# Projections issued in four parts with an attention unit behind three of them, another order of chunks, and one modulation row summed by VectorE

## The reference

```
mod   = silu(cond) @ w_mod + b_mod          # six rows of 2048 for each of the two conditions: SH1 SC1 G1 SH2 SC2 G2
h     = rms_norm(x) * (1 + SC1) + SH1
z     = h @ w_in                            # columns: queries, keys, values of the head groups A, B, C
o     = attention(A: 6 heads), windowed attention with a sink(B: 6 heads), latent attention(C: 4 heads)
x1    = x + G1 * (concat(o) @ w_o)
h2    = rms_norm(x1) * (1 + SC2) + SH2
y     = x1 + G2 * experts(h2)               # top-1 group, top-2 of its 8 experts; each expert silu(h2@w1)*(h2@w3) @ w2
```

## Time and profile before

| | us |
|---|---|
| median of 3 runs | 1692.17 (1691.69 to 1693.72) |
| the profiled execution | 1693.61 |
| its span, first to last instruction | 1691.8 |
| PE busy, whole span | 1591.9 (94%) |
| DVE busy | 690.1 (41%) |
| ACT busy | 263.7 (16%) |
| POOL busy | 106.1 (6%) |

### The profile page before, as it was taken

One profiled execution on the slowest core, in us unless ns is written; L12 is line 12 of the kernel. 1 busy time (PEld: TensorE's weight loads), 2 busy tenths in 40 slices (PEclk: granted clock), 3 DMA queues, 4 the chain that ended last, 5 costly groups with the idle time before them and its releaser, 6 DMA issues.

```text
span 1691.8 us, 18209 instructions
## 1 busy us (share of the span) xinstructions
PE 1591.9 (94%) x6671; PEld 655.4 (39%) x6716; DVE 690.1 (41%) x1361; ACT 263.7 (16%) x706; POOL 106.1 (6%) x192
## 2 busy tenths in 40 slices
PE   5999999999999999999999998999999999998998
PEld 3455555544434444443332332333233233233332
DVE  3113232113245893344444345345344433544444
ACT  2004221112133000011101101110110111111010
POOL 1022100100020100000000000000000000000000
PEclk9999999999999999999999999999999999999999
DMA  9992643535199765599999999999999999999995
GB/s 394 420 385 120 230 193 119 215 109 213 54 368 410 275 264 221 203 366 426 427 429 428 428 425 428 428 424 428 427 426 428 425 424 427 428 428 423 428 427 237
DMA packets 60526, 581.94 MB, mean 344 GB/s; under 512 B 9129, under 2 KB 10121, under 8 KB 16105
## 3 DMA queue, kind: packets, MB, share of 16 engines
q1 hardware_dynamic: 53120, 557.34, 79.6%
q0 software_dynamic: 6064, 23.22, 3.6%
q10 hardware_dynamic: 1296, 0.77, 0.2%
HBM read 584.06 MB, written 7.05 MB: 349 GB/s over the span
## 4 chain that ended last, share of the span: by engine, by line
PE 68%; DMA 17%; DVE 4%; issue 2%; ACT 1%; SPq 0%; POOL 0%; ACTq 0%
PE bank L1298 24%; DMA ring<-in_w 17%; PE bank L1046 14%; PE bank L1208 7%; PE bank L1025 7%; DVE r L1794 2%; PE bank L920 2%; PE bank L1331 2%; PE bank L1133 2%; PE bank L1257 2%; PE bank L1280 1%; PE bank L1108 1%; PE bank L1194 1%; PE bank L1116 1%; PE bank L1313 1%
## 5 line engine op out<-in xcount | busy, mean ns | idle before, releaser
L1298 PE MATMUL bank<-ring,r 128*64 128x512 f32 x1920 | 469.6, 619 | 45.5 <-DMA ring<-in_w 45.5
L1298 PEld LDWEIGHTS bank<-ring,r 128*64 128x64 f32 x1920 | 129.6, 140 | 303.3 <-issue 303.3
L1046 PE MATMUL bank<-ring,r 128*128 128x384 f32 (+1 forms) x672 | 242.4, 519 | 0.0
L2014 DVE TENSOR_TENSOR bank<-bank,r 128x512 f32<-128x512 f32 x180 | 125.9, 700 | 266.2 <-PE bank L1208 266.2
L1331 PE MATMUL bank<-ring,mod_row 128*64 128x512 f32 x896 | 195.4, 593 | 7.9 <-ACT mod_row L1547 7.9
L1025 PE MATMUL bank<-ring,r 128*128 128x512 f32 x384 | 170.0, 595 | 0.0
L1046 PEld LDWEIGHTS bank<-ring,r 128*128 128x128 f32 x672 | 126.9, 191 | 103.7 <-issue 44.7
L1208 PE MATMUL bank<-r 128*128 128x512 bf16 x495 | 137.6, 382 | 7.2 <-issue 7.2
L2016 DVE TENSOR_TENSOR r<-r,bank 128x512 f32<-128x512 f32 x180 | 123.7, 687 | 6.2
L1331 PEld LDWEIGHTS bank<-ring,mod_row 128*64 128x64 f32 x896 | 75.4, 137 | 118.2 <-issue 107.9
L1208 PEld LDWEIGHTS bank<-r 128*128 128x128 bf16 x540 | 38.0, 97 | 167.4 <-DVE r L2016 97.4
(11 more groups left out here) (281 smaller groups left out, 1238.4 us busy)
## 6 DMA issues: line engine op xcount, KB each, us to landing
ring<-in_w SPq DMA_DIRECT2D x180, 2048.0 KB, 17.8
ring<-in_w_mod SPq DMA_DIRECT2D x64, 1024.0 KB, 11.8
ring<-in_w_first SPq DMA_DIRECT2D x32, 1024.0 KB, 25.9
ring<-in_w SPq DMA_DIRECT2D x19, 1024.0 KB, 9.7
ring<-in_w_o SPq DMA_DIRECT2D x16, 1024.0 KB, 6.2
r<-mod_d POOLq DMA_DIRECT2D x8, 1024.0 KB, 8.0
ring<-in_w_aq SPq DMA_DIRECT2D x8, 768.0 KB, 11.4
ring<-in_w_bq SPq DMA_DIRECT2D x8, 768.0 KB, 13.0
```

The source lines that it names most:

```text
L1046: mm = pe.matmul(acc[acc_of(a)][:, 0:w], h_t[:, k, t * P:(t + 1) * P], wu[:, j, :], start=(k == 0), stop=(k == KD - 1))
L1298: mm = pe.matmul(ps[64 * c:64 * c + 64, :], xg_t[:, j, 64 * c:64 * c + 64], big_cut(slot_of(u), (8, 512))[:, j % 8, :], start=(j == 0), st ...
L2014: v.tensor_tensor(ps[:, :], ps[:, :], g2b[:, min(t, 1), cols], ALU.mult).then_inc(strip_scaled, 1)
```

## The change

It has four parts.

1. The order of chunks is now aq0, aq1, akv, bkv, bq0, bq1. A job of aq0 to bq1 is issued in four parts of its sum (the four ring units), and between the parts stand attention units, one behind each of the first three (`woven`). Units of C go with aq0 and aq1, of A with bkv and bq0, the first nine of B with bq1. The second nine of B stay behind all jobs, each of the first seven with two mod steps ahead of it (one for the seventh). The turn of an earlier job stands behind the first part, ahead of the first unit, and the norm right behind the job.
2. The row SH2 is no longer computed by mod steps. DVE adds its 16 units (`sh2_step`), mostly one for each job, behind the second unit; PE folds the sums (`fold_sh2`), DVE copies them out, POOL stores them. G1 takes SH2's place as the first row of the mod steps.
3. The two sums lie in two slots of `ring`, which are taken out of the circular order at the end of the first stage and come back ten units after the fold (`ring_plan`, `emptied`); meanwhile the ring has ten slots. POOL clears them and loads the bias there.
4. The places where a slot's number is worked out are changed accordingly.

```diff
-          ("aq0", Q_A, 384), ("aq1", Q_A + 384, 384), ("bq0", Q_B, 384),
-          ("akv", K_A, 512), ("bq1", Q_B + 384, 384), ("bkv", K_B, 512)]
+          ("aq0", Q_A, 384), ("aq1", Q_A + 384, 384), ("akv", K_A, 512),
+          ("bkv", K_B, 512), ("bq0", Q_B, 384), ("bq1", Q_B + 384, 384)]
...
-LATER_GROUPS = (SH2, G1, SC2)
+LATER_GROUPS = (G1, SH2, SC2)
...
-def ring_slot(m):
-
-    return (m + RING_FROM) % SLOTS
+def ring_plan(n, held_from, held_to):
+
+    def run(names):
+        at, prior, order, last, held = [], [], list(names), {}, []
+        for m in range(n):
+            if m == held_from:
+                held, order = order[:2], order[2:]
+            if m == held_to:
+                order = held + order
+            s = order.pop(0)
+            order.append(s)
+            at.append(s)
...
+    def sh2():
+        k = next(summed)
+        units.append(("mod", SH2, k))
+        steps.append(("sh2", k))
+
+    held_to = []
+
+    def fold():
+        steps.append(("fold", SH2))
+        held_to.append(len(units) + SLOTS - 2)
...
+    def woven(what, *between):
+
+        jobs.append(what)
+        n = len(jobs) - 1
+        for i in range(4):
+            steps.append(("part", n, i))
+            if i == 0 and len(pending) == 2:
+                turn()
+            for do in between[i] if i < len(between) else ():
+                do()
+        steps.append(("proj", n))
+        steps.append(("norm", n))
+        pending.append(n)
...
+            elif (name, t) == ("aq0", 0):
+                woven((name, t), (), (sh2,))
+            elif name == "aq0":
+                woven((name, t), (of("C", t - 1, 0),), (of("C", t - 1, 1), sh2), (of("C", t - 1, 2), mod1))
...
+            elif (name, t) == ("bkv", 0):
+                woven((name, t), (of("A", 0, t),), (of("A", 1, t), sh2), (of("A", 2, t), mod1, turn))
+            elif name in ("bkv", "bq0"):
+                h = 0 if name == "bkv" else SHARE
+                woven((name, t), (of("A", h, t),), (of("A", h + 1, t), sh2), (of("A", h + 2, t), mod1))
...
+            elif t == 0:
+                woven((name, t), (of("B", 0, t),), (of("B", 1, t), sh2), (of("B", 2, t), ))
+            elif t == 1:
+                woven((name, t), (of("B", 0, t),), (of("B", 1, t), fold), (of("B", 2, t), mod1))
...
-    attend("B", range(SHARE), fill=later[:SHARE * TILES])
-    attend("B", range(SHARE, HEADS_B), fill=later[SHARE * TILES:] + [("lead", 0), ("lead", 1)])
...
+    for n, (t, h) in enumerate((t, h) for t in range(TILES) for h in range(SHARE, HEADS_B)):
+        if n < 7:
+            mods(2)
+        else:
+            lead(n - 7)
+        attend("B", h, t)
+        if pending:
+            turn()
...
+        def emptied(m):
+
+            if m >= held_to and prior[m] < held_from and slots[m] in held:
+                return row_out, 2 * 32
+            return frees[prior[m]]
...
+            def fold_sh2():
+
+                pe.wait_ge(*frees[unit_no[("mod", SH2, KD - 1)]])
+                pe.wait_ge(mod_read, 1)
+                for c in range(2):
+                    for q in range(4):
+                        mm = pe.matmul(mod_ps[32 * q:32 * q + 2, :], K("sel")[:, c:c + 2], sh2_sum[c][:, q * 512:(q + 1) * 512],
...
+                    if i == 0:
+                        acc_wait(a)
+                    m = unit_no[("in", name, i)]
+                    arrived(m)
+                    wu = cut(slots[m], (4, w))
+                    for j in range(4):
+                        k = 4 * i + j
+                        mm = pe.matmul(acc[acc_of(a)][:, 0:w], h_t[:, k, t * P:(t + 1) * P], wu[:, j, :],
+                                       start=(k == 0), stop=(k == KD - 1))
+                    if i == 3:
+                        mm.then_inc(acc_full, 1)
+                        a += 1
...
+            def sh2_step(k):
+
+                m = unit_no[("mod", SH2, k)]
+                if k == 0:
+                    v.wait_ge(sh2_rows_in, 2 * 16)
+                v.wait_ge(*full_of(m))
+                for c in range(2):
+                    if c and k:
+                        v.wait_ge(*frees[unit_no[("mod", SH2, k - 1)]])
+                    last = v.scalar_tensor_tensor(out=sh2_sum[c], in0=ring[:, slots[m], :], scalar=csil[:, k, c:c + 1],
+                                                  in1=sh2_sum[c], op0=ALU.mult, op1=ALU.add)
+                    if c == 0:
+                        after(last)
+                last.then_inc(*done_of(m))
...
+                elif s[0] == "fold":
+                    v.wait_ge(mod_done, 2)
+                    v.tensor_copy(sh2_sum[0][:, 0:512], mod_ps[:, :]).then_inc(mod_read, 1)
...
+            for slot in held:
+                g.wait_ge(*frees[max(m for m in range(held_from) if slots[m] == slot)])
+            g.memset(sh2_sum[0], 0.0)
+            after(g.memset(sh2_sum[1], 0.0))
+            for c in range(2):
+                g.dma_start(sh2_sum[c][0:1, :], b_rows[SH2:SH2 + 1]).then_inc(sh2_rows_in, 16)
...
+                elif s[0] == "fold":
+                    g.wait_ge(mod_read, 2)
+                    for c in range(2):
+                        g.dma_start(mod_d[SH2, c].rearrange("(q n) -> q n", q=4), sh2_sum[0][c:P:32, 0:512]).then_inc(row_out, 16)
```

More of the change, by code:

```diff
@@ L167, in plan, with mods, lead, turn @@
     units = []
[L169 to L176, removed]
     for i in range(4):
         units.extend(("first", g, i, m) for g in FIRST_GROUPS for m in range(4))
[L180 to L197, removed]
+    later = [(g, k) for g in LATER_GROUPS if g != SH2 for k in range(KD)]
+    summed = iter(range(KD))
+    pending, scored, unnormalised, turned_p = [], [], [], []
+    def mods(n):
+        for g, k in later[:n]:
+            units.append(("mod", g, k))
+            steps.append(("mod", g, k))
+        del later[:n]
+    def sh2():
[6 more added lines that the diff above has]
+        held_to.append(len(units) + SLOTS - 2)
+    def lead(i):
+        if i == 0:
+            units.extend([("out", 0, j) for j in range(4)])
+        steps.append(("lead", i))
+    def turn():
+        steps.append(("turn", pending.pop(0)))
+    def advance(u=None):
         if u is not None:
@@ L215, in advance, with attend, job, of @@
                 turned_p.append(done)
[L217 to L234, removed]
+    def attend(*what):
+        atts.append(what)
+        advance(len(atts) - 1)
+    def job(kind, what):
+        jobs.append(what)
+        steps.append((kind, len(jobs) - 1))
+        steps.append(("norm", len(jobs) - 1))
+        if len(pending) == 2:
+            turn()
+        pending.append(len(jobs) - 1)
+    def woven(what, *between):
+        jobs.append(what)
+        n = len(jobs) - 1
[8 more added lines that the diff above has]
+        pending.append(n)
+    def of(group, h, t):
+        return lambda: attend(group, h, t)
+    def mod1():
+        mods(1)
     for t in range(TILES):
@@ L242, in plan @@
         for t in range(TILES):
-            attends = (name == "aq0" and t > 0) or (name == "aq1" and t < 2) or name in ("bq1", "bkv")
-            job("proj", (name, t), norm=not attends)
-            n = len(jobs) - 1
             if name == "cq1":
+                for i in range(4):
+                    steps.append(("part", len(jobs), i))
+                job("proj", ("cq1", t))
                 if t == 0:
@@ L269, in plan @@
[L269 to L281 removed]
+                job("kvc", ("kvc", t + 1, 0))
```

160 lines of the change are left out of this document (78 added, 82 removed).

## The result

| | median us | ratio to before, 95% interval |
|---|---|---|
| before | 1691.99 (19 runs) | |
| changed | 1695.62 (1691.08 to 1697.94, 19 runs) | 1.0017 [1.001, 1.0024] |

The change makes the kernel 3.6 us slower where 13 us less were forecast. One execution of experiment 2 took 2766.9 us at a mean granted clock of 0.59 and is left out of that experiment's ratio.

What follows compares the result with a forecast made beforehand. PE was taken to bound attention and output, weight loads the second half. Terms -14.1 - 11.8 - 1.7 + 10.6 + 1 + 3 = -13.0 us gave 1680.6 us for the profiled execution, 1679 us as median; range 1664 to 1691 us.

Steps and rivals of the forecast that it cites:

- 16 steps less the fold, clock: Attention stage: 16 SH2 mod steps leave PE, a fold comes, net -14.1 us; slow clock near 376 us goes, -1.7 us.
- PE idle before: Attention stage: PE's 11.8 us of idle time go, since projection parts between units cover DVE's and ACT's answers.
- twelve turn waits: In 12 jobs, scores right behind a turn wait for ACT's copy, 0.8 or 0.93 us each: +10.6 us, bounds 0 and 19.
- a wait here and there: Attention stage: what idle time is left, the drain at the end of B and occasional waits: +1 us.
- ring at the end: End of attention: PE waits for the last SC2 loads with ten slots, +3 us, bounds 0 and 8.
- output stage: Stage behind attention: G2's sum and PE's fold move along with attention's end, length unchanged.
- DVE's 17 us per job: Three-head job: PE takes 17 to 18 us; DVE needs about 13.4 of 17 for wait, norm, units and additions.
- the 1.7 us of 376 us: Before, behind two waits at 376 us, a job ran at first at clock 0.51; these 1.7 us were to be saved.
- 21 us for twelve drops: Clock rival: each of 12 new pauses behind a turn lowers PE's clock, 12 x 1.75 = 21 us, 1700 us; chance 0.04.
- the rival of DVE in the way: At each of 12 jobs' third unit PE waits out DVE's additions, 2.1 us each, 25 us: 1704 us; chance 0.07.
- 20.4 and 18 us: End of attention: seven last SC2 units landed at 20.4 us, PE reaching the seventh after about 18 us.
- Twelve turn waits of 1.4 us: Starved-at-the-end rival: turns cost 1.4 us each, +17 instead of +10.6, SC2 loads +8: 1690 us; chance 0.11.

Runs made afterwards that it cites:

- experiment 2: Changed kernel with the turn behind the first attention unit of a job instead of ahead of it: 1695.49 us, ratio 1.002.
- 6: Changed order with SH2 again as 16 mod steps on PE where DVE's additions stood, no fold, twelve slots: 1706.03 us, ratio 1.0085.
- 4: Changed kernel with both turn and norm behind the first unit of a job: 1679.67 us, ratio 0.992.
- 3: Changed kernel with DVE's norm of aq0, aq1, bkv, bq0, bq1 jobs behind the next job's first unit: 1688.39 us, ratio 0.9977.
- 5: Changed kernel with only half the columns of 13 SC2 units loaded: 1685.58 us, ratio 0.9964.
- 8: Kernel of experiment 4 with mod steps spread over B's last nine units, output projection starting earlier, five G2 units ahead of output's third block: 1675.22 us, ratio 0.9899.
- 1 (one profile): Changed kernel again without edit, with a profile of another execution: 1695.84 us, ratio 1.0019.
- experiment 9: Changed kernel with 14 products by zeros on PE ahead of six instructions for which it waited: 1691.96 us, ratio 0.9995.
- experiment 10: Kernel of experiment 8 with four products by zeros ahead of three of PE's waits: 1676.35 us, ratio 0.9897.

## Why the prediction was wrong

The sum by its own steps, for the profiled executions, and then for the medians:

| step | forecast us | found us | shown by |
|---|---|---|---|
| PE busy: 16 steps less the fold, clock | -14.1 - 1.7 | -13.6 | stages; 6 |
| PE idle before | -11.8 | -11.8 | stages |
| twelve turn waits | +10.6 | +7.7 | waits; 4 |
| a wait here and there (8.1 behind the norm) | +1 | +8.7 | waits; 2, 3 |
| ring at the end | +3 | +4.2 | waits; 5 |
| output stage | 0 | +2.2 | landmarks; 8 |
| start of the stage, experts | 0 | +0.9 - 0.9 | landmarks |
| rest | 0 | +0.1 | |
| profile to profile | -13.0 | -2.5 | |
| typical execution, changed | 0 | +4.5 | 1 (one profile) |
| before's profile above its median | 0 | +1.6 | runs |
| median to median | -13 | +3.6 | |

**The step that failed** is "with 2.6 us of projection between two units, DVE and ACT have their answer ready ... Left over are the drain at the end of B and a wait here and there, 1 us". I had worked out that DVE's norm starts 2.7 us behind its job and takes 2.74 us, and counted both against DVE's 17 us per job, as if they could lie anywhere. But the change put the norm right behind the job in DVE's order; before, it stood behind three units, and in the earlier trace rows it started 6.9 us after the root was there. Right behind the job the 2.7 us are a block: DVE idles for POOL's root (3.89 us at 212 to 216), and the next unit's maximum, copy and division wait behind it, and ACT's copies behind those. That is 8.1 of the 8.7 us of waits where I had 1; moving the norm alone brought 7.4 us (experiment 3), and the additions cause none of it (experiment 6). The prediction asked whether DVE has time enough and not what is queued behind its waiting instruction.

**The clock** is the second. I had the 1.7 us of 376 us come back and gave 21 us for twelve drops the chance of 0.04, because single pauses had left the stage at 1.00. What came is between: 6.75 us at most in the fastest execution and 11.5 in another, behind pauses of 1.18 us and more, though not behind all of them. The turn waits of 0.57 to 0.73 us have no drop of their own behind them in the profile after. Already in the fastest execution the loss is larger than the 2.2 us by which PE's busy time shrank less than forecast, and the one further profile puts the 4.5 us between the best execution and the typical one down to the clock as well. That these drops go when PE has work in the pauses is shown by experiment 9; that the spread of the executions comes from them is not, since it stayed at 4.9 us there.

**Right were** the worth of the sums on DVE: 10 us net of the ring in the changed order and 8.7 in the better one, against 14.1 - 3; that PE takes no wait from the additions (experiment 6), so the rival of DVE in the way had the right engine and the wrong instruction; the number of the turn waits and about their size (7.7 us measured, 8.7 by experiment 4, 10.6 forecast); and that the experts take as long as before, to within 0.9 us. The ring's starvation was in the right place and too small: 4.2 to 5.0 us in waits, and 10 us with the clock behind them and what follows (experiment 5). The forecast of 3 us was the small difference of two times, 20.4 and 18 us, and 2 us of the first stand in no row of this case.

Some readings were off without deciding anything. DMA is full from the eighteenth slice on, not the nineteenth, and also in the twelfth and thirteenth, where the ring was short. Two transposes of a turn take about 0.29 us by the earlier trace rows, two thirds of 0.43, and not 0.22. Twelve turn waits of 1.4 us are 17 us, not 19. The loads of the earlier trace rows began 87 us ahead of the stage's end, not 88.

**Left open** is why the bias rows came late in the output stage, which moved the residual and cost the 2.2 us. They were used 6.8 us after POOL had issued their loads, with DMA at 1.02 in that time, 4.6 us with 0.97 before, and 2.7 us with 0.47 in experiment 8; it was 6.9 us in experiment 6, which has neither the sums of SH2 on DVE nor the two kept slots. That the time follows what else passes DMA is likely and not shown, since no run changed that alone. Why the clock falls behind one pause and not behind another, in two executions or in one, is open as well.

## What to carry to other kernels

When a step is moved, look on every engine at what its waiting instruction now stands in front of: an engine with half its time free still makes the critical one wait if an instruction that is not ready heads its queue. Remove waits in the order in which they cover one another: the turn's move was worth 0.3 us alone and 8.7 us after the norm's. Count with a pause of TensorE what the clock may cost behind it, here about 1.7 us for a drop, and spread what a full DMA must bring; time saved ahead of a stretch with DMA full can return as a wait for it, as in experiment 10.

## What the runs showed of the hardware

One program's executions differ by 6.9 us (1691.08 to 1697.94), and their mean granted clock goes with it (of the 19, 0.984 to 0.986 for the five shortest, 0.981 for the two longest); two that were profiled have the same waits within 1 us. Behind a pause of 1.18 us, eight records of a projection took 4.42 instead of 2.75 us, and 2.75 us behind pauses of 1.17 us at 241.93 us and of 2.53 us at 282.02 us; two of 3.15 and 0.84 us left the clock at 0.50 over five us. Filling such pauses with products by zeros won 3.8 us.
